# One layer of S5, block attention, memory attention and a conv FFN on one core: two PSUM banks each for scores and transposes, another order of the attention loop, and S5 parts behind projection tiles

## The chip, the core and the metric

The program runs on one core of one Trainium2 chip. The metric is the device time of one execution in microseconds, as the median of several runs. TensorE (PE) multiplies, its weight loads are listed apart as PEld, VectorE is DVE, ScalarE is ACT, GpSimd is POOL, SyncE (SP) issues most transfers. The granted TensorE clock was 1.00 of full speed over the whole execution.

## What is computed

Everything is fp32, for 512 tokens of width 1024. The reference, cut to what matters here:

```python
def reference(x, mem, ...):
    h = x
    hn = rms_norm(h, norm_mix)
    proj = hn @ w_in                       # u (512) | q | k | v (each 8 heads x 64)
    q, k = rms_norm(q, attn_qn), rms_norm(k, attn_kn)
    y_ssm = s5_mixer(u, ...)               # 32 groups x 16 channels, state 64, complex diagonal
    y_att = moba_attention(q, k, v, rel_bias)
    mixed = concat([rms_norm(y_ssm, gnorm_ssm), rms_norm(y_att, gnorm_attn)])
    h = h + mixed @ w_out
    h = h + memory_cross_attention(rms_norm(h), rms_norm(mem), ...)   # 4 heads x 128, 256 memory rows
    h = h + conv_ffn(rms_norm(h), ...)     # width 2816, causal depthwise conv of 3, silu gate

def s5_mixer(u, ...):
    # s[t] = ab * s[t-1] + bb @ u[t] ;  y = Re(c @ s) + d * u
    y = gelu(y)
    return y * sigmoid(y @ w_glu + b_glu)
```

With 512 tokens and blocks of 256, all earlier blocks are selected, so moba_attention is causal attention with a bias by distance bucket.

## The kernel before

Five programs are written out by hand, one for each engine (sync, gpsimd, scalar, vector, tensor). Each runs in its written order; semaphores hold them together. No scheduler moves anything.

**Weights.** They arrive in chunks of 1 MB (two units) in two raw buffers. ACT rounds a unit to its high part (`split_hi`, line 485), DVE forms the rest (`split_lo`, line 496, counted by the semaphore `lo_done`), into a ring of four units. A product of 128x128 by 512 columns is three matmuls (lines 513 to 515). The small fp32 matmuls of S5 and attention are line 1771, transposes on PE line 1774. `A_` (line 882) is any activation on ACT; `tt` and `stt` (lines 1253, 1259) are two-operand operations on DVE. A chunk is fetched into a raw buffer once both halves of the units in it are done.

**PSUM.** `plan()` (lines 273 to 328) names every use of the eight banks in order with `use(bank, name)`. PE's `fill(name)` waits until the bank's previous use was drained, the readers' `read(name)` until it is full. Before, scores of head step s (`sc{s}`) go round banks 3, 4 and 5; the transposed probabilities (`pt{s}`) of all steps, and the row factors `rl{t}`, use bank 6; attention's values (`pv{t}`) use bank 7. Banks 0, 1 and 2 hold the memory projections (`mk`, `mv`), the four pieces of the GLU product (`z0` to `z3`), and the output pieces `g{t}{half}` in bank (2t + half) mod 3. So g00 is in bank 0 and g01 in bank 1.

**S5.** The recurrence is cut into chunks of eight tokens. For each quarter q of the groups PE does `states_in(q)` (needs u, written to HBM and gathered back: semaphore `u0_in`), `kernels_in(q)` (needs a table of powers that POOL makes in `ca_table(q)`, line 804: `ca_ready`) and later `outputs(q, a)`. They stand between the projections of q, k and v, `proj(u, ...)`, each of four tiles (`proj_tile`, six matmuls of 512 columns). On POOL a chain of small operations on the S5 parameters opens the program; ca_table(0) ends it. DVE's `split_lo(0)` is ahead of its copy of the transposed parameters (`lam`), on which PE's next transposes wait.

**Attention.** There are 32 head steps, s = 8t + head, in tiles t of 128 query rows. For step s PE makes scores (`scores(s)` does s and s+1), DVE adds the bias and takes the extremum (`logits`, line 1555), ACT takes the exponential into `pbuf` (`probabilities`), PE transposes it in t+1 blocks (`prob_transposes`), ACT (even s) or DVE (odd s, line 383) copies that to SBUF (`pt_evac`), and PE multiplies with v (`values(s)` does s and s+1). PE's loop takes two steps at a time, a pair. At the head of a pair other work is inserted: `mv_tile` (memory values, up to s=6), `glu_half` (s = 8, 10, 12, 14: z0 to z3), and from s=16 pieces of the first half of the output projection (`sout_piece`, table `SOUT_AT`). ACT takes tanh of z{m} at s-1 = `GLU_AT[m]`; DVE makes the gated y (`y2`) at s-2 and its low part (`lo_of`) at s-4, ACT its high part and square at s-3. POOL sums squares. At step 19 these sums are reduced on PE, and DVE turns them into the root-mean-square factor (`mean_sq`, `root("ss")`). `g_residual(n)` on DVE scales g{t}{half} by it, adds it to the residual stream (which needs its transfer, `h_in`) and frees the bank. `G_ADD_AT` gives the steps of the first six. `SPLIT_AT` gives the steps at which weight units are split.

Of the kernel before, what the change touches and what calls it, by code (L numbers as in the profile page):

```python
# [20 lines left out]
TT = T // 128  # L21
# [5 lines left out]
H, HD = 8, 64  # L27
# [21 lines left out]
for _n, _k in GAINS:  # L49
# [14 lines left out]
SS_AT, MK_ROWS_AT = 19, 2  # L64

SOUT_AT = [(16, 0, 0), (16, 0, 1), (18, 1, 0), (20, 0, 2), (20, 0, 3), (22, 1, 2), (22, 1, 1), (24, 1, 3), (24, 2, 0),
           (26, 2, 2), (26, 2, 1), (28, 2, 3), (28, 3, 0), (30, 3, 1), (30, 3, 2), (30, 3, 3)]
G_ADD_AT = [21, 21, 23, 25, 27, 29]

# [31 lines left out]
def layer(nc, A, out):  # L101
# [10 lines left out]
    with ctx:  # L112
# [160 lines left out]
        def plan():  # L273
# [21 lines left out]
            for s in range(TT * H):  # L295
                if s >= H and s % H == 0:
                    use(6, f"rl{s // H - 1}")
                use(3 + s % 3, f"sc{s}"); use(6, f"pt{s}")
            for t in range(TT):
                use(7, f"pv{t}")  # L300
            use(6, "rl3"); use(6, "sa")
            use(0, "mk0"); use(1, "mk1"); use(0, "mv0"); use(1, "mv1")
            use(2, "z0"); use(0, "z1"); use(1, "z2"); use(2, "z3")
            use(5, "kx0"); use(3, "kx1")
            for t in range(TT):
# [376 lines left out]
        def _(pool):  # L682
# [36 lines left out]
            def ts(o, a, s1, s2, o1, o2):  # L719
                return nc.gpsimd.tensor_scalar(o, a, s1, s2, o1, o2)  # L720

            c = lambda i: sp[:, i, :]
            ab_re, ab_im, a_im = pw[:, 0, :, 1], pw[:, 1, :, 1], lam[:, GP:2 * GP]
# [149 lines left out]
        def _(act):  # L873
# [222 lines left out]
            mem_rows("mk", mkrow, 0)  # L1096
            probabilities(0)
            y_out(3)
            mem_rows("mk", mkrow, 1)
            for s in range(TT * H):  # L1100
                if s % 2 == 1:
                    pt_evac(act, lambda o, i: A_(o, i, ACT.Copy), s - 1)
                if s + 1 < TT * H:
                    probabilities(s + 1)
                if s >= H and s % H == 0:
                    factors_in(s // H - 1)
# [135 lines left out]
        def _(dve):  # L1242
# [103 lines left out]
            def turns(step):  # L1346
# [10 lines left out]
                if step == 3:  # L1357
# [6 lines left out]
                          lsrow[:, :].unsqueeze(2).to_broadcast([GP, 2, NS])).then_inc(step_row, 1)  # L1364
            split_lo(dve, 0)
            p = read(dve, "lam")
# [3 lines left out]
            x_half_lo(0, LOW)  # L1370
            x_half_lo(0, HIGH)
            split_lo(dve, 1)
            x_half_lo(1, LOW)
# [188 lines left out]
            for s in range(TT * H):  # L1562
# [7 lines left out]
                if s == SS_AT + 1:  # L1570
                    drained(V.tensor_copy(ev(sq, "ss"), p[:, 384:384 + TT]), f"pt{SS_AT}")
                    after_drain(dve, f"pt{SS_AT}")
                    mean_sq("ss")
                if s > H and s % H == 2:
                    ya_scale(s // H - 1)
# [13 lines left out]
                if s - 2 in GLU_AT:  # L1589
                    m = GLU_AT.index(s - 2)  # L1590
                    after_drain(dve, f"z{m}")
                    stt(yT[:, m, :], sg[:, m, :], 1.0, yT[:, m, :], ALU.add, ALU.mult).then_inc(y2_ready, 1)
                if s == SS_AT + 2:
                    root("ss")
                    dve.wait_ge(h_in, 16 * TT)
                for n, at in enumerate(G_ADD_AT):
# [172 lines left out]
        def _(pe):  # L1769
# [215 lines left out]
            proj(5, U_Q, "q")  # L1985
            states_in(0)
            kernels_in(0)
            proj(6, U_Q, "q")
            proj(7, U_Q, "q")
# [24 lines left out]
            for t in range(TT):  # L2014
                proj_tile(14, U_V, "v", t)
                outputs(2, t)
            weights_in(3)
# [125 lines left out]
            for s in range(0, TT * H, 2):  # L2143
# [7 lines left out]
                for at, t, i in SOUT_AT:  # L2151
                    if at == s:
                        sout_piece(t, i)
                if s >= H and s % H == 0:
                    factors(s // H - 1)
                if s + 2 < TT * H:
                    scores(s + 2)
                prob_transposes("pt", "sc", s, s // H + 1, 4)
                if s >= 2:
                    values(s - 2)  # L2160
                prob_transposes("pt", "sc", s + 1, s // H + 1, 4, s + 1 != SS_AT)
# [201 lines left out]
```

## Time and profile before

| | us |
|---|---|
| median of 3 runs | 717.7 (717.35 to 719.49) |
| the profiled execution | 719.06 |
| its span in the trace | 717.5 |
| PE busy | 698.7 |
| DVE busy | 423.7 |
| ACT busy | 308.0 |
| POOL busy | 130.7 |

A row of a timeline gives the start in us from the start of the span, the duration, engine and line, operation, result<-operands, the shape, how many like operations it groups, and in brackets how long the engine was idle just before, and on what it waited. A matmul's duration contains its fill and drain, so the cost of one in a row of them is the distance between two starts. A shape such as 64\*128 is the part of the array that the matmul uses.

In time the program goes: loading and transposing of x and the parameters to 13, projection and S5 to about 160, the attention loop to about 250, the output projection and memory attention, and from about 370 the FFN.

### The profile page before, as it was taken

The page shows a single profiled execution, that of the slowest core. Times are in us where ns is not written, and L with a number is a line of the kernel's source. Part 1 is how long each engine was busy: PE and PEld are TensorE (multiplying, and loading weights), DVE is VectorE, ACT ScalarE, POOL GpSimd, SP SyncE. Part 2 cuts the span into 40 slices and gives each one's busy share as a digit, 9 for nine tenths or more (in the row PEclk, how much of TensorE's full clock was granted, in tenths as well). Part 3 has the DMA queues.
Part 4 walks back from the last instruction along what each step waited for, and adds up shares of the span by engine and source line. Part 5 has one row for each costly group of instructions (what it writes and reads, how often), then busy time and mean ns, then how long its engine had stood idle before and what let it go on. Part 6 is the DMA issues. An engine that isn't in the chain of part 4 may idle for free.

```text
span 717.5 us, 10849 instructions
## 1 busy us (share of the span) xinstructions
PE 698.7 (97%) x3913; PEld 576.6 (80%) x3913; DVE 423.7 (59%) x710; ACT 308.0 (43%) x515; POOL 130.7 (18%) x134
## 2 busy tenths in 40 slices
PE   8999999998999999999999999999999999999998
PEld 7968887885676887878898888888888887888886
DVE  4998957737576567684856555554555574333333
ACT  5736444457664546253654333334333442232220
POOL 2999975023031110100200000000000000000000
PEclk9999999999999999999999999999999999999999
DMA  8645433266410033011124232232232332331203
GB/s 250 215 130 124 149 104 106 66 215 212 169 59 1 1 147 112 7 59 59 60 65 155 74 117 91 84 117 76 99 117 65 111 117 66 111 117 60 115 1 117
DMA packets 62999, 73.95 MB, mean 103 GB/s; under 512 B 20873, under 2 KB 47796, under 8 KB 62836
## 3 DMA queue, kind: packets, MB, share of 16 engines
q1 hardware_dynamic: 59172, 66.12, 28.4%
q10 hardware_dynamic: 3792, 7.36, 3.2%
q8 instruction: 22, 0.36, 0.2%
q14 instruction: 13, 0.11, 0.0%
HBM read 68.08 MB, written 5.78 MB: 103 GB/s over the span
## 4 chain that ended last, share of the span: by engine, by line
PE 81%; DVE 5%; ACT 4%; POOL 4%; DMA 2%; issue 2%; SPq 2%; ACTq 0%; DVEq 0%; POOLq 0%
PE pb L513 24%; PE pb L515 23%; PE pb L514 23%; PE pb L1771 7%; PE pb L1774 4%; POOL F L691 2%; DMA raw<-in_w_in 1%; ACT F L882 1%; DVE F L1253 1%; SPq L616 1%; ACT xs L882 1%; DMA F<-scr_b 1%; DVE xs L1259 1%; DVE F L1259 1%; ACT wring L485 1%
## 5 line engine op out<-in xcount | busy, mean ns | idle before, releaser
L496 DVE TENSOR_TENSOR wring<-raw,wring 128x1024 fp32r<-128x1024 f32 x100 | 128.5, 1287 | 76.6 <-ACT wring L485 76.3
L513 PE MATMUL pb<-xs,wring 128*128 128x512 f32 (+1 forms) x448 | 165.1, 368 | 0.2 <-issue 0.2
L515 PE MATMUL pb<-xs,wring 128*128 128x512 f32 (+1 forms) x448 | 164.1, 366 | 0.0
L514 PE MATMUL pb<-xs,wring 128*128 128x512 f32 (+1 forms) x448 | 164.1, 366 | 0.0
L485 ACT ACTIVATE wring<-raw 128x1024 fp32r<-128x1024 f32 x100 | 105.0, 1054 | 88.2 <-PE pb L515 75.0
L1259 DVE SCALAR_TENSOR_TENSOR F<-pb,ccol,F 128x511 f32<-128x511 f32 x88 | 65.9, 749 | 103.4 <-ACT F L882 97.5
L513 PE MATMUL pb<-wring,bs 128*128 128x512 f32 x240 | 96.3, 401 | 2.1 <-ACT F L882 1.2
L513 PEld LDWEIGHTS pb<-xs,wring 128*128 128x128 f32 x448 | 84.5, 189 | 14.2 <-issue 0.6
L515 PEld LDWEIGHTS pb<-xs,wring 128*128 128x128 f32 x448 | 84.5, 189 | 13.6
L514 PEld LDWEIGHTS pb<-xs,wring 128*128 128x128 f32 x448 | 84.5, 189 | 13.6
L515 PE MATMUL pb<-wring,bs 128*128 128x512 f32 x240 | 93.6, 390 | 0.0
L514 PE MATMUL pb<-wring,bs 128*128 128x512 f32 x240 | 93.5, 390 | 0.0
L882 ACT ACTIVATE F<-pb,ccol 128x512 f32<-128x512 f32 x44 | 34.2, 778 | 121.4 <-PE pb L515 117.5
L513 PE MATMUL pb<-wring,xs 128*128 128x512 f32 x192 | 81.0, 422 | 2.4 <-DVE F L1259 1.6
L1771 PE MATMUL pb<-F 64*128 64x128 f32 (+7 forms) x864 | 73.9, 276 | 2.2 <-DMA F<-scr_u 1.2
L515 PE MATMUL pb<-wring,xs 128*128 128x512 f32 x192 | 75.3, 392 | 0.0
L514 PE MATMUL pb<-wring,xs 128*128 128x512 f32 x192 | 75.1, 391 | 0.0
L1771 PEld LDWEIGHTS pb<-F 64*128 64x128 f32 (+3 forms) x864 | 59.4, 157 | 15.6 <-issue 9.5
L882 ACT ACTIVATE F<-pb 128x256 f32<-128x256 f32 (+6 forms) x60 | 26.7, 470 | 69.8 <-PE pb L1774 52.1
L513 PEld LDWEIGHTS pb<-wring,bs 128*128 128x128 f32 x240 | 45.1, 188 | 12.8 <-ACT F L882 2.0
L515 PEld LDWEIGHTS pb<-wring,bs 128*128 128x128 f32 x240 | 45.0, 188 | 9.7
L514 PEld LDWEIGHTS pb<-wring,bs 128*128 128x128 f32 x240 | 45.1, 188 | 8.7
(142 smaller groups left out, 777.7 us busy)
## 6 DMA issues: line engine op xcount, KB each, us to landing
raw<-in_ffn_w_up SPq DMA_DIRECT2D x22, 1024.0 KB, 5.0
raw<-in_ffn_w_down SPq DMA_DIRECT2D x11, 1024.0 KB, 4.8
F<-in_x SPq DMA_DIRECT2D x8, 512.0 KB, 5.0
raw<-in_w_in ACTq DMA_DIRECT2D x4, 1024.0 KB, 5.7
raw<-in_w_out SPq DMA_DIRECT2D x4, 1024.0 KB, 5.3
raw<-in_w_in SPq DMA_DIRECT2D x3, 1024.0 KB, 5.9
raw<-in_x_wkv ACTq DMA_DIRECT2D x3, 1024.0 KB, 5.8
raw<-in_x_wq SPq DMA_DIRECT2D x2, 1024.0 KB, 5.2
```

Source lines behind the costliest of these rows:

```text
L485: ins = nc.scalar.activation(w_unit(u, 0), raw_unit(u), ACT.Copy)
L496: ins = nc.vector.tensor_tensor(w_unit(u, 1), raw_unit(u), w_unit(u, 0).bitcast(f32), ALU.subtract)
L513: nc.tensor.matmul(ps, lh, rh, start=first, stop=False)
L514: nc.tensor.matmul(ps, lh, rl_, start=False, stop=False)
L515: return nc.tensor.matmul(ps, ll, rh, start=False, stop=last)
L616: sync.dma_start(toep[d * CG:(d + 1) * CG, :, (L - 1 - d) * CG:], kt[0:CG, :, 0:(d + 1) * CG]).then_inc(t_in[q], 16)
L691: return nc.gpsimd.tensor_tensor(o, a, b, ALU.mult)
L882: return nc.scalar.activation(o, i, f, **k)
L1253: return V.tensor_tensor(o, a, b, op)
L1259: return V.scalar_tensor_tensor(out=o, in0=a, scalar=s1, in1=b, op0=o1, op1=o2)
L1771: return nc.tensor.matmul(o, l, r, start=start, stop=stop)
L1774: return nc.tensor.transpose(o, i, ident[0:i.shape[0], 0:i.shape[0]])
```

## The change

Six things are altered.

1. **Banks.** Scores go round banks 3 and 4, transposes round 5 and 6. mv0 is in bank 2 and mv1 in bank 0; z0 to z3 are in banks 1, 2, 0, 1; the memory keys' transposes are in 3 and 4. The g pieces keep their banks, so the use before g01 in bank 1 is now z3 (before: z2), and the one before g00 in bank 0 is z2 (before: z1).
2. **ACT** takes the exponentials of a pair directly after each other, at odd s.
3. **PE's pair**: values(s-2) and scores(s+2) come first behind the inserted work, then the factors, then both transposes.
4. **DVE** does root("ss") at s=20 instead of 21, and g00's and g01's residuals too.
5. **split_lo(0)** is done by POOL, at the head of its program.
6. **S5**: states_in(0) and kernels_in(0) come after the first tile of proj(6), outputs(2,0) after tile 1 of unit 14, directly ahead of outputs(2,1).

```diff
-G_ADD_AT = [21, 21, 23, 25, 27, 29]
+G_ADD_AT = [20, 20, 23, 25, 27, 29]
...
-                use(3 + s % 3, f"sc{s}"); use(6, f"pt{s}")
+                use(3 + s % 2, f"sc{s}"); use(5 + s % 2, f"pt{s}")
...
-            use(0, "mk0"); use(1, "mk1"); use(0, "mv0"); use(1, "mv1")
-            use(2, "z0"); use(0, "z1"); use(1, "z2"); use(2, "z3")
-            use(5, "kx0"); use(3, "kx1")
+            use(0, "mk0"); use(1, "mk1"); use(2, "mv0"); use(0, "mv1")
+            use(1, "z0"); use(2, "z1"); use(0, "z2"); use(1, "z3")
+            use(3, "kx0"); use(4, "kx1")
...
+            pool.wait_ge(hi_done, 1)
+            nc.gpsimd.tensor_tensor(w_unit(0, 1), raw_unit(0), w_unit(0, 0).bitcast(f32), ALU.subtract)\
+                .then_inc(lo_done, 1)
...
             probabilities(0)
+            probabilities(1)
             y_out(3)
...
-                if s + 1 < TT * H:
+                if s % 2 == 1 and s + 1 < TT * H:
                     probabilities(s + 1)
+                    probabilities(s + 2)
...
-            split_lo(dve, 0)
             p = read(dve, "lam")
...
+            dve.wait_ge(lo_done, 1)
             split_lo(dve, 1)
...
                     mean_sq("ss")
+                    root("ss")
+                    dve.wait_ge(h_in, 16 * TT)
...
-                if s == SS_AT + 2:
-                    root("ss")
-                    dve.wait_ge(h_in, 16 * TT)
...
-            states_in(0)
-            kernels_in(0)
-            proj(6, U_Q, "q")
+            for t in range(TT):
+                proj_tile(6, U_Q, "q", t)
+                if t == 0:
+                    states_in(0)
+                    kernels_in(0)
...
                 proj_tile(14, U_V, "v", t)
-                outputs(2, t)
+                if t == 1:
+                    outputs(2, 0)
+                if t >= 1:
+                    outputs(2, t)
...
-                if s >= H and s % H == 0:
-                    factors(s // H - 1)
-                if s + 2 < TT * H:
-                    scores(s + 2)
                 prob_transposes("pt", "sc", s, s // H + 1, 4)
-                if s >= 2:
-                    values(s - 2)
                 prob_transposes("pt", "sc", s + 1, s // H + 1, 4, s + 1 != SS_AT)
```

(The added lines of the last piece stand ahead of the two transposes: values(s-2), scores(s+2), factors.)

What PE runs behind the output pieces of the pair s=16, before (scores are the rows with a result of 128x128 from F, values those with 64x128, the row factors the transposes of F, the transposes of step 16 and 17 those of pbuf):

```order
L1774 MATMUL pb<-ident,F 128x128 [waits bank_free6,rlrow_ready]
L1774 MATMUL pb<-ident,F 128x128 x3
L1771 MATMUL pb<-F 128x128 [waits bank_free4,bank_free3]
L1771 MATMUL pb<-F 128x128 x5
L1774 MATMUL pb<-ident,pbuf 128x128 [waits bank_free6,bank_free4]
L1774 MATMUL pb<-ident,pbuf 128x128 x2
L1771 MATMUL pb<-F 64x128 [waits bank_free6]
L1771 MATMUL pb<-F 64x128 x3
L1774 MATMUL pb<-ident,pbuf 128x128 [waits bank_free6,bank_free5]
L1774 MATMUL pb<-ident,pbuf 128x128 x2
```

and after:

```order
L1775 MATMUL pb<-F 64x128 [waits bank_free6,bank_free5]
L1775 MATMUL pb<-F 64x128 x3
L1775 MATMUL pb<-F 128x128 [waits bank_free4,bank_free3]
L1775 MATMUL pb<-F 128x128 x5
L1778 MATMUL pb<-ident,F 128x128 [waits bank_free6,rlrow_ready]
L1778 MATMUL pb<-ident,F 128x128 x3
L1778 MATMUL pb<-ident,pbuf 128x128 [waits bank_free5,bank_free3]
L1778 MATMUL pb<-ident,pbuf 128x128 x2
L1778 MATMUL pb<-ident,pbuf 128x128 [waits bank_free6,bank_free4]
L1778 MATMUL pb<-ident,pbuf 128x128 x2
```

The values moved from between the two transposes to the front, and wait for the drains of both banks of transposes; the two transposes stand together and fill different banks.

ACT around s=13 to 15, before (the exponentials write pbuf and lsum, the tanh of z2 and z3 are the ones with hbglu):

```order
L882 ACTIVATE F<-pb6 128x256 [waits bank_full6,pv_done]
L882 ACTIVATE pbuf,lsum<-pb5,nmx 128x256 [waits logit_ready,bank_full5,bank_full6]
L485 ACTIVATE wring<-raw 128x1024 [waits bank_full0,raw_in0]
L882 ACTIVATE F<-pb1,hbglu 128x512 [waits bank_full1]
L882 ACTIVATE xs<-F,gcol 128x512 [waits y2_ready]
L882 ACTIVATE F<-F 128x512
L882 ACTIVATE pbuf,lsum<-pb3,nmx 128x256 [waits logit_ready,bank_full3,bank_full6]
L882 ACTIVATE F<-pb6 128x256 [waits bank_full6,pv_done]
L882 ACTIVATE pbuf,lsum<-pb4,nmx 128x384 [waits logit_ready,bank_full4,bank_full6]
L882 ACTIVATE F<-pb2,hbglu 128x512 [waits bank_full2]
```

and after:

```order
L885 ACTIVATE F<-pb5 128x256 [waits bank_full5,pv_done]
L885 ACTIVATE pbuf,lsum<-pb3,nmx 128x256 [waits logit_ready,bank_full3,bank_full5]
L885 ACTIVATE pbuf,lsum<-pb4,nmx 128x256 [waits logit_ready,bank_full4,bank_full6]
L485 ACTIVATE wring<-raw 128x1024 [waits bank_full2,raw_in0]
L885 ACTIVATE F<-pb0,hbglu 128x512 [waits bank_full0]
L885 ACTIVATE xs<-F,gcol 128x512 [waits y2_ready]
L885 ACTIVATE F<-F 128x512
L885 ACTIVATE F<-pb5 128x256 [waits bank_full5,pv_done]
L885 ACTIVATE pbuf,lsum<-pb3,nmx 128x384 [waits logit_ready,bank_full3,bank_full5]
L885 ACTIVATE pbuf,lsum<-pb4,nmx 128x384 [waits logit_ready,bank_full4,bank_full6]
L885 ACTIVATE F<-pb1,hbglu 128x512 [waits bank_full1]
```

Each odd step now has two exponentials, and the tanh of z3 (last row) stands behind both of its step; it reads bank 1.

PE at the end of proj(5), before:

```order
L1771 MATMUL pb<-F 64x64 [waits bank_free5,bank_free4,u0_in]
L1771 MATMUL pb<-F 64x64 x7
L1771 MATMUL pb<-F 64x64 [waits bank_free5]
L1771 MATMUL pb<-F 64x64 x7
L1771 MATMUL pb<-F 16x128 [waits bank_free7,bank_free6,ca_ready]
L1771 MATMUL pb<-F 16x128 x15
L513 MATMUL pb<-wring,xs 128x512 [waits lo_done]
```

and after:

```order
L513 MATMUL pb<-wring,xs 128x512 [waits lo_done]
L514 MATMUL pb<-wring,xs 128x512
L515 MATMUL pb<-wring,xs 128x512
L513 MATMUL pb<-wring,xs 128x512
L514 MATMUL pb<-wring,xs 128x512
L515 MATMUL pb<-wring,xs 128x512
L1775 MATMUL pb<-F 64x64 [waits bank_free5,bank_free4,u0_in]
L1775 MATMUL pb<-F 64x64 x7
L1775 MATMUL pb<-F 64x64 [waits bank_free5]
L1775 MATMUL pb<-F 64x64 x7
L1775 MATMUL pb<-F 16x128 [waits bank_free7,bank_free6,ca_ready]
L1775 MATMUL pb<-F 16x128 x15
```

Six matmuls of 512 columns, one tile, moved ahead of the states and kernels.

## Rows read from the trace of the kernel before

**Rows 1.** the page's busy line (engine, us, share of the span, instructions).

```profile
PE 698.7 (97%) x3913; PEld 576.6 (80%) x3913; DVE 423.7 (59%) x710; ACT 308.0 (43%) x515; POOL 130.7 (18%) x134
```

**Rows 2.** PE's waits by releaser: total us, times, longest.

```profile
PE pb L1774 <- ACT F L882: 2.9, 6, 1.0
PE pb L513 <- DVE F L1259: 2.0, 2, 1.6
```

**Rows 3.** PE's timeline, S5 part: start, us, operation, count, [idle before <-releaser].

```profile
50.88 0.39 PE L515 MATMUL pb<-wring,xs 128*128 128x512 f32 x1
52.45 1.15 PE L1771 MATMUL pb<-F 128*64 128x64 f32 x32 [1.18 <-DMA F<-scr_u]
53.83 1.92 PE L1771 MATMUL pb<-F 64*16 64x128 f32 x32 [0.23 <-POOL F L804]
...
122.25 0.39 PE L514 MATMUL pb<-wring,xs 128*128 128x512 f32 x1
122.48 0.40 PE L515 MATMUL pb<-wring,xs 128*128 128x512 f32 x1
123.47 1.22 PE L1771 MATMUL pb<-F 128*128 128x64 f32 x12 [0.59 <-DVE bs L1259]
```

**Rows 4.** POOL's timeline, last of ca_table(0).

```profile
51.50 2.28 POOL L804 TENSOR_TENSOR F<-F 128x576 f32<-128x576 f32 x1
```

**Rows 5.** the start: DVE, PE, POOL, ACT; last, POOL's halves grouped (min/median/max ns).

```profile
10.13 1.23 DVE L496 TENSOR_TENSOR wring<-raw,wring 128x1024 fp32r<-128x1024 f32 x1 [4.40 <-ACT wring L485]
...
11.52 1.75 PE L1774 MATMUL pb<-ident,F 128*128 128x128 f32 x14 [0.82 <-DVE lam L1367]
...
14.99 1.05 POOL L720 TENSOR_SCALAR sp<-sp 128x16 f32<-128x16 f32 x1
...
16.06 1.28 ACT L882 ACT_TABLE_LOAD   x1
...
L828 POOL TENSOR_TENSOR xs<-F,xs x4: 1274/1280/1297, 157.6 to 178.5; 128x512 fp32r<-128x512 f32 x4
```

**Rows 6.** PE's timeline in the attention loop.

```profile
163.10 0.50 PE L513 MATMUL pb<-wring,bs 128*128 128x512 f32 x1 [1.18 <-ACT F L882]
...
179.36 0.47 PE L513 MATMUL pb<-xs,wring 128*128 128x512 f32 x1
...
185.36 0.41 PE L1774 MATMUL pb<-ident,pbuf 128*128 128x128 f32 x2 [1.02 <-ACT F L882]
...
189.09 0.44 PE L1774 MATMUL pb<-ident,pbuf 128*128 128x128 f32 x2
189.46 0.66 PE L1771 MATMUL pb<-F 128*64 128x128 f32 x8
190.15 0.41 PE L1774 MATMUL pb<-ident,pbuf 128*128 128x128 f32 x2
190.32 0.47 PE L513 MATMUL pb<-xs,wring 128*128 128x512 f32 x1
...
205.21 0.52 PE L1774 MATMUL pb<-ident,pbuf 128*128 128x128 f32 x3 [0.78 <-ACT F L882]
...
220.32 0.50 PE L513 MATMUL pb<-wring,xs 128*128 128x512 f32 x1 [1.56 <-DVE F L1259]
```

**Rows 7.** DVE's timeline in the attention loop.

```profile
177.91 0.28 DVE L383 COPY F<-pb 128x128 f32<-128x128 f32 x1
...
198.10 1.76 DVE L1259 SCALAR_TENSOR_TENSOR F<-F 128x512 f32<-128x512 f32 x1
199.78 1.21 DVE L496 TENSOR_TENSOR wring<-raw,wring 128x1024 fp32r<-128x1024 f32 x1
```

**Rows 8.** ACT's timeline in the attention loop.

```profile
195.15 1.06 ACT L485 ACTIVATE wring<-raw 128x1024 fp32r<-128x1024 f32 x1
...
201.64 0.58 ACT L882 ACTIVATE pbuf<-pb,nmx 128x384 f32<-128x384 f32 x1 [1.82 <-DVE nmx L1555]
202.21 0.68 ACT L882 ACTIVATE F<-pb,hbglu 128x512 f32<-128x512 f32 x1
```

More of the change, by code:

```diff
@@ L2153, in _ @@
                         sout_piece(t, i)
+                if s >= 2:
+                    values(s - 2)
+                if s + 2 < TT * H:
+                    scores(s + 2)
                 if s >= H and s % H == 0:
                     factors(s // H - 1)
-                if s + 2 < TT * H:
-                    scores(s + 2)
                 prob_transposes("pt", "sc", s, s // H + 1, 4)
-                if s >= 2:
-                    values(s - 2)
                 prob_transposes("pt", "sc", s + 1, s // H + 1, 4, s + 1 != SS_AT)
```

## The prediction

> **What bounds the kernel now.** I first read the page's busy line [rows 1]: PE is busy 698.7 of the span's 717.5 us. So only two things can move the time: PE's idle (the other 18.8 us) and what PE pays for its own order. Next I read PE's waits grouped by releaser [rows 2]: behind the start, the largest groups wait for ACT (2.9 us) and for a DVE sum (2.0). Then I read PE's timeline at each of those waits, to see which instruction is late and who is behind it. Two places matter. In the S5 part PE stands still for 1.18 us ahead of the states, 0.23 ahead of the kernels and 0.59 ahead of outputs(2,0) [rows 3]. In the attention loop it waits 1.18, 1.02, 0.78 and 1.56 us [rows 6]; smaller ones are in the 2.9 of [rows 2]. The stretch behind the loop (the FFN above all) is untouched. Durations are from the profiled execution (719.06 us, span 717.5); the sum is a difference and is laid on the median of 717.7, 1.4 us below that execution. A measurement of this kernel can tell about 0.3% (2.15 us) from no change.
>
> **S5 parts behind tiles.** Before, states_in(0) stands at PE's front from 51.27 to 52.45, waiting for the gathered u [rows 3]. After, the six products of tile (6,0) go first. One costs 0.23 us from start to start (122.25 to 122.48, [rows 3]), so the tile is 1.37 us; it ends at 52.6 and the wait is filled. The states (1.15 us) then end at 53.8, when ca_table on POOL has just finished (51.50 + 2.28 = 53.78, [rows 4]), so the 0.23 goes too. Saved: 1.18 + 0.23 = 1.41, less the 0.03 by which the tile overshoots the wait: **−1.38**. What hides it is a tile whose operands lie ready; if POOL came later by x, x less 0.2 would come back. The later outputs(2,0) now stands behind tile (14,1), whose 1.37 us cover the 0.59 of [rows 3] and the 0.17 by which the step (122.48 to 123.47) further exceeds a product's 0.23. One change of tile shape less gives at most 0.15 more: **−0.76 to −1.0**, I take −0.92, near its upper end because outputs(2,0) and (2,1) now follow each other. Evacuations of these parts move with PE. S5 together: **−2.3**.
>
> **split_lo(0) on POOL.** DVE's took 1.23 us and PE's next work waited 0.82 for the copy behind it [rows 5]. POOL's own subtractions of half that size take 1.28 [rows 5], so POOL needs some 2.55 from 10.1 to 12.65. DVE's lam copy then comes at once, and the first products could start about 0.3 earlier than 13.03, since they need POOL's result only in their third matmul. But POOL's parameter chain, whose first part ended at 14.99 + 1.05 = 16.04, then starts 0.75 us later. ACT loads its table from 16.06 to 17.34 [rows 5], and only then can it take that result: if the load does not wait for it, the 0.75 lies beside the load. PE meets two points that do not move with it, u at 52.4 and ca_table at 53.8, and the 0.3 is lost there: **0**. Bounds: −0.3, and +0.75 if POOL's whole chain moves, since the kernels then wait for POOL. A rule of the Trainium skill speaks against this part: page "SBUF — State Buffer", section "Who interferes with whom", says that a VectorE instruction with two SBUF inputs contends with a GpSimd instruction that reads SBUF, and the loser waits. No run here shows that pair of instructions yet; by this rule POOL's subtraction would end later than 12.65, and what it adds comes on top of the 0.75.
>
> **Attention: the early steps.** Giving mv1 bank 0 instead of 1 takes away the 1.18 at 163.10 [rows 6], since nothing that ACT is still to read is in it. With two banks for transposes the second transpose of a pair no longer waits for the evacuation of the first. But values(s−2) now open the block behind the products, and need the evacuation of pt(s−1). For values(4) that is DVE's copy at 177.91, which ends at 178.19 [rows 7], behind skip_in(3) and split_lo(25); values(4), scores(8), two transposes of step 6 and of 7 follow (about 1.3 us). The pair of s=8 thus starts at about 179.4, as before (179.36, [rows 6]). All gain up to there, some 2 us, is given back: **0**. From s=8 to 14 the waits of 1.02 [rows 6] and the cheaper order count: PE is 1.0 ahead at s=16.
>
> **The cheaper order.** Two transposes in front of values take 0.37 us (189.09 to 189.46), and the same two in front of full products 0.17 (190.15 to 190.32) [rows 6]. With pt(s) directly ahead of pt(s+1), a pair pays that exit once less: 0.15 (if half of the difference is an overlap that returns elsewhere, 0.1; at most 0.2), in about 15 pairs −2.2. Part of it stands in the 1.0 at s=16. The Trainium skill's page "TensorEngine Tiling (Array Packing)", Key Properties, says that changing the tiling mode drains TensorE; [rows 6] agree with some 0.2 us. By that rule values to scores is still a change, so a pair keeps three of four; were all four charged alike, the saving would be the same one of 0.15 to 0.2.
>
> **The new wait.** The second piece at s=16 fills bank 1. Before, its last reader was the tanh of z2; after, that of z3. On ACT that tanh (202.21 before, [rows 8]) stands at s=15 behind pt_evac(14), prob(16) and now also prob(17). Going through the queues: PE finishes pt(13) at 194.3; ACT does prob(14), prob(15), split_hi(28) (1.06, [rows 8]), tanh z2 and the first xs to 198.0; DVE follows with lo_of (0.7), y2 (1.76 beside POOL, [rows 7]), split_lo(28) (1.21, [rows 7]) and both logits to 202.6; ACT's two exponentials and the tanh (0.58 + 0.58 + 0.68, [rows 8]) end at 203.7 to 204.5. PE, 1.0 ahead, wants the bank at 200.6. Wait: **3.1 to 3.9, I take 3.4**. It replaces the 0.78 at 205.21 [rows 6] and one of 0.2 behind it, as both probabilities are then done. So at s=18: −1.0 + 3.4 − 1.0 = +1.4; a wait of values(16) for step 17's evacuation, bounded by 0 and the 0.78 at 205.21, adds 0.6 (nearer to that row, as its copy too stands behind logits): +2.0.
>
> **The early root.** g11 at 220.32 waited 1.56 for g00's sum on DVE, which stood behind the root at s=21 [rows 6]; moved to s=20 it is in time, with 0.16 more as the step shrinks: −1.72, leaving +0.3. Behind it DVE's queue holds the logits(22), 1.5 us later, which nobody wants before 216. The pairs from s=22 on give five times 0.15, less 0.2 for a transpose bank behind rl: −0.55. **Attention: −0.3.** Behind the loop nothing changes. Sum: −2.3 − 0.3 = **−2.6, or 715.1 us**.
>
> **Rivals.**
>
> *A, the early gain lasts.* If DVE's queue before 177.91 moves forward with PE (its split_lo(25) waits for ACT, which is freed by the 1.18, and not for the transfer that skip_in(3) needs), the 2.0 us at s=8 stay, and every later time comes 2.0 sooner, the new wait's too. If y2 also takes the 0.75 that DVE's other 512-column sums take, and not 1.76, the new wait is 1.0 shorter: −2.6 − 2.0 − 1.0 = −5.6, 712.1. For it: the whole loop is driven from PE. Against: the copy of [rows 7] ends a queue that DVE works off without a gap from 173.6.
>
> *B, the pair chain becomes the bound, and it is slower.* Scores, both logits, both exponentials, both transposes now go as one group; in pairs 16 to 22 ACT and DVE also carry squares, xs, y2, the root and two residuals. Each of three pairs then waits 1.7 us more, the length of one y2 [rows 7]: +5.1 − 2.6 = +2.5, 720.2. It decides from 0.87 a pair (2.6/3). For it: the 0.78 at 205.21 shows PE already waiting for ACT there [rows 6]; against: between 206.8 and 218.6 PE waits for neither of them.
>
> *C, the S5 gain fails* because split_lo(0) delays POOL's chain by 0.75 or more up to ca_table: S5 −0.5, sum −0.8, 716.9. For it: POOL's chain was on the path (0.23, [rows 3]); against: the table load's cover.
>
> *D, the edit doesn't do what it says* (the order stays in effect because every second bank waits for the same reader): −2.3 from S5 alone, 715.4, within the forecast's own range.
>
> **How the numbers follow.** Forecast with D 0.56, A 0.15, C 0.15, B 0.14. The forecast's own range is 713.0 to 717.3: S5 ±0.5, the bank wait −0.3/+0.5, the order ±0.7, values(16) ±0.4. To leave out no more than 2 in 10, the range goes down past A's 712.1 by its own half-width, to 710.9, and up to part of B, 719.2. Faster by over 0.3% is below 715.55: A's 0.15 and 0.34 of the forecast: 0.49. Slower is above 719.85: 0.09 of B, whose middle is 720.2, and 0.05 for the upper tails of C and of the forecast: 0.14. The same: 0.37.
>
> **What would show it.** Tile (6,0) from 51.0 and no idle ahead of the states or kernels; outputs(2,0) without idle; mv1 without its 1.18; s=8 at the old time less S5's gain; a wait of 3 to 4 us for ACT at the second piece of s=16; no 1.56 at g11. Wrong if POOL's ca_table ends after 54.0, if the bank wait is under 1 or over 6 us, or if new waits stand ahead of values in many pairs.

## The result and the profile after

The changed kernel takes **722.23 us** (median of 9 runs, 720.21 to 724.75), the kernel before 718.02 (9 runs beside it). The ratio is **1.0063**, with a 95% interval of 1.0050 to 1.0076: slower by 4.5 us, where 2.6 us less was forecast and the range ended at 719.2. The profiled execution has a span of 721.7 us, against 717.5. One execution of the kernel before, beside the last four experiments, took 1153.44 us at a mean granted clock of 0.558; it stands in no ratio here.

The S5 part went as planned. These rows of PE's timeline answer to [rows 3]: PE does the tile, the states follow with no idle, and the kernels wait 0.15 us for POOL instead of 0.23; outputs(2,0) and (2,1) run as one group of 24 with no idle ahead of them, where 0.59 was.

```profile
52.02 0.39 PE L515 MATMUL pb<-wring,xs 128*128 128x512 f32 x1
52.34 1.15 PE L1775 MATMUL pb<-F 128*64 128x64 f32 x32
53.65 1.92 PE L1775 MATMUL pb<-F 64*16 64x128 f32 x32 [0.15 <-POOL F L807]
...
122.52 2.33 PE L1775 MATMUL pb<-F 128*128 128x64 f32 x24
```

POOL's last operation of ca_table(0), which answers to [rows 4], ends at 53.59:

```profile
51.31 2.28 POOL L807 TENSOR_TENSOR F<-F 128x576 f32<-128x576 f32 x1
```

Where PE waits now (the view of its waits by releaser, as [rows 2]: total us, times, longest):

```profile
PE pb L1775 <- DVE F L383: 4.8, 4, 1.6
PE pb L513 <- ACT F L885: 3.7, 1, 3.7
PE pb L1778 <- ACT F L885: 1.5, 4, 0.6
PE pb L1775 <- DVE F L1258: 1.4, 1, 1.4
```

The old entries are gone or smaller: 1.18 ahead of mv1, 1.02 at s=8, 1.56 at g11 [rows 6]. In their place stand 4.8 us for DVE's copy of transposed probabilities (line 383), 1.4 us for a DVE product (line 1258) and one wait of 3.7 us for ACT. PE's timeline in the loop places them; 202.66 is the second output piece at s=16, and the rows of line 1775 with a wait are all values:

```profile
168.93 0.86 PE L1775 MATMUL pb<-F 128*64 128x128 f32 x8 [0.92 <-DVE F L383]
...
174.53 1.08 PE L1775 MATMUL pb<-F 128*64 128x128 f32 x12 [1.60 <-DVE F L383]
...
176.20 0.63 PE L514 MATMUL pb<-xs,wring 128*128 128x512 f32 x1
176.62 0.63 PE L515 MATMUL pb<-xs,wring 128*128 128x512 f32 x1
...
179.70 0.39 PE L514 MATMUL pb<-xs,wring 128*128 128x512 f32 x1
179.93 0.40 PE L515 MATMUL pb<-xs,wring 128*128 128x512 f32 x1
...
202.66 0.47 PE L513 MATMUL pb<-wring,xs 128*128 128x512 f32 x1 [3.72 <-ACT F L885]
...
211.89 1.74 PE L1775 MATMUL pb<-F 128*64 128x128 f32 x24 [1.37 <-DVE F L1258]
...
224.13 1.97 PE L1775 MATMUL pb<-F 128*64 128x128 f32 x28 [0.83 <-DVE F L383]
...
231.08 1.97 PE L1775 MATMUL pb<-F 128*64 128x128 f32 x28 [1.41 <-DVE F L383]
```

One thing in these rows is no wait. Two products of 512 columns start 0.42 us apart at 176.20 to 176.62, and 0.23 apart at 179.70 to 179.93. The view by stretches tells why (columns: from:to, us, busy us and instructions of PE, of its weight loads, of DVE, ACT and POOL, then granted clock, DMA share, GB/s):

```profile
172.00:175.50 3.50, 1.90 (x17) 1.17 (x15) 2.38 (x4) 1.57 (x2) 1.77 (x2) 1.00 1.01 379
175.50:179.30 3.80, 3.80 (x14) 2.98 (x12) 1.09 (x6) 3.16 (x7) 1.12 (x2) 0.55 1.02 415
198.00:202.50 4.50, 0.94 (x5) 0.42 (x3) 3.45 (x8) 1.79 (x6) 0.98 (x2) 1.00 0.00 0
202.90:206.80 3.90, 3.90 (x22) 2.63 (x23) 2.44 (x2) 0.75 (x2) 1.32 (x1) 0.56 0.02 4
```

The clock granted to TensorE is 1.00 up to 175.5, 0.55 from there to 179.3, and 1.00 again behind it; and 0.56 from 202.9 to 206.8. Those are the two levels, 2.4 and 1.2 GHz, with the edges of the stretch mixed in. Each time PE had stood still just before: it was busy for 1.90 of the 3.5 us before the first fall (after 0.92 and 1.60 us of waiting), and for 0.94 of 4.5 before the second (3.72). In the kernel before the whole span has 1.00, though it too waits 1.56 at one place [rows 6].

Put against the old timeline, the pair of s=0 starts 2.43 us earlier than before (156.19, before 158.62), s=2 4.85, s=4 5.17, s=8 3.6 earlier (175.74, [rows 6] 179.36), s=10 2.5, s=16 2.85 earlier (197.28, before 200.13). Then s=18 is 2.1 late, s=20 3.4, s=26 3.7, s=30 3.4, and the end 4.2.

### The profile page after: what moved, and what is told of

The parts are those of the page before. It is cut to its first block, busy times and chain, and to the rows that moved or that the text cites. A ratio compares the mean times of both kernels' runs of the same rounds, so it can differ in the third digit from the quotient of the medians.

```text
span 721.7 us, 10851 instructions
## 1 busy us (share of the span) xinstructions
PE 700.1 (97%) x3913; PEld 579.3 (80%) x3913; DVE 422.9 (59%) x709; ACT 308.3 (43%) x515; POOL 132.8 (18%) x135
## 4 chain that ended last, share of the span: by engine, by line
PE 81%; DVE 7%; ACT 4%; POOL 4%; issue 2%; DMA 1%; SPq 0%; ACTq 0%; DVEq 0%; POOLq 0%
PE pb L513 24%; PE pb L515 23%; PE pb L514 23%; PE pb L1775 8%; PE pb L1778 4%; POOL F L691 2%; DVE F L1258 1%; DMA raw<-in_w_in 1%; DVE wring L496 1%; ACT F L885 1%; ACT pbuf L885 1%; DVE wring L499 1%; ACT xs L885 1%; DVE xs L1264 1%; ACT wring L485 1%
## 5 line engine op out<-in xcount | busy, mean ns | idle before, releaser
L1775 PE MATMUL pb<-F 64*128 64x63 f32 (+7 forms) x864 | 73.6, 278 | 6.5 <-DVE F L383 4.8
```

The costliest lines, as they stand in the source:

```text
L1775: return nc.tensor.matmul(o, l, r, start=start, stop=stop)
```

## The experiments

All are timed against the kernel before on the same chip, side by side; its median was 717.7 us beside the first eight experiments and 718.7 beside the last four. The changed kernel was not timed again beside them, so a distance "less than the changed kernel" is a difference of medians from 722.23, and good to about 1 us; where it matters the difference of the ratios is given. Two theories stood at the start. **Theory 1**: the wait for the tanh of z3, and the clock behind it, are the loss. **Theory 2**: PE's new order in a pair closes a loop through DVE, and that loop is the loss.

**The S5 parts alone.** Part 6 put into the kernel before:

```diff
-            states_in(0)
-            kernels_in(0)
-            proj(6, U_Q, "q")
+            for t in range(TT):
+                proj_tile(6, U_Q, "q", t)
+                if t == 0:
+                    states_in(0)
+                    kernels_in(0)
...
-                outputs(2, t)
+                if t == 1:
+                    outputs(2, 0)
+                if t >= 1:
+                    outputs(2, t)
```

> The kernel before, with part 6 alone (states_in(0) and kernels_in(0) behind the first tile of proj(6), outputs(2,0) behind tile 1 of unit 14). If the S5 gain is real and lasts to the end, the span is 2.3 us shorter than before, about 715.4 as a median, with no idle of PE ahead of the states and of outputs(2,0). Rival: attention's waits (1.18, 1.02, 0.78, 1.56) grow by what PE gained, since they are set by ACT and DVE, and the end moves by under 1 us.

Measured: 715.57 us, ratio 0.9972 (0.9960 to 0.9983), so 2.0 us. It lasts to the end: the rows of attention moved forward as a block, with the same waits:

```profile
181.18 0.41 PE L1774 MATMUL pb<-ident,pbuf 128*128 128x128 f32 x2 [1.02 <-ACT F L882]
...
201.15 0.52 PE L1774 MATMUL pb<-ident,pbuf 128*128 128x128 f32 x3 [0.78 <-ACT F L882]
...
216.25 0.50 PE L513 MATMUL pb<-wring,xs 128*128 128x512 f32 x1 [1.55 <-DVE F L1259]
```

They are 1.02, 0.78 and 1.55, at times 4.1 us ahead of [rows 6]. Of the 4.1, 0.9 is where this execution began (10.62 against the 11.52 of [rows 5]); the block of the last mk and first mv products starts 3.2 ahead (155.43, before 158.62), so 2.3 are the S5 parts'; and that block, up to the scores, took 0.96 less in this execution (5.11 us from 155.43 to 160.54, before 6.07 from 158.62 to 164.69), 0.67 of it at mv1's wait (0.51, before 1.18). The waits that were left did not grow, so the rival is out.

**split_lo(0) on POOL, added to that** (parts 5 and 6):

> The same, and split_lo(0) on POOL too (parts 5 and 6). If part 5 is worth nothing, the time is that of s5_only within 0.4 us; if POOL's chain is late by 0.75, PE waits ahead of the kernels and the time is up to 0.75 longer; if the earlier start lasts, 0.3 shorter.

Measured: 714.75 us, 0.9964 (0.9951 to 0.9977), 0.6 us better than s5_only by the ratios, within both intervals. POOL took 2.37 us for the subtraction. Its parameter chain then began at 11.77, where s5_only has 11.07, but the operation behind ACT's table load ran at 17.04, where s5_only has 16.98: the load hid all but 0.06 of the 0.70. DVE's group of eight operations, whose first ran beside the subtraction, took 3.22 us, in s5_only 3.23. Whether the gain of the start lasts cannot be told at this resolution; no cost shows.

So everything else, parts 1 to 4, costs 722.2 − 714.8 = 7.5 us (7.1 by the ratios), where the forecast had them at −0.3.

**PE's old order in a pair**, the rest as changed:

```diff
-                if s >= 2:
-                    values(s - 2)
-                if s + 2 < TT * H:
-                    scores(s + 2)
                 if s >= H and s % H == 0:
                     factors(s // H - 1)
+                if s + 2 < TT * H:
+                    scores(s + 2)
                 prob_transposes("pt", "sc", s, s // H + 1, 4)
+                if s >= 2:
+                    values(s - 2)
                 prob_transposes("pt", "sc", s + 1, s // H + 1, 4, s + 1 != SS_AT)
```

> The changed kernel with PE's old order in a pair (factors, scores, transposes of s, values, transposes of s+1), everything else as changed. If the waits ahead of values (1.0 and 1.6 at s=4 and 6, 1.4, 0.8 and 1.4 from s=18 on) come from values standing first, they shrink to under 0.5 each, the first clock dip at 175 to 179 us goes with them (1.6 us), and a pair costs 0.15 more: about 3 us faster than the changed kernel. If the waits are set by DVE's queue whatever PE does, they stay, at the second transposes, and the time is the changed kernel's plus 1 to 2 us.

Measured: 714.59 us, 0.9958 (0.9945 to 0.9972). That is 7.6 us faster than the changed kernel, more than twice what was expected. Without the order of part 3 none of the loss is left, and what it costs is larger than the waits ahead of values that it shows (6.1 us). The profiled execution of this kernel is its slowest (720.46 us, seven of the other eight are between 714.36 and 715.28): a transfer of the S5 outputs came late in it, DVE stood for it 2.46 us, PE 4.20 behind that, and the clock fell there, and again behind the wait for the tanh. That wait is still 3.15 us.

**The bank of g01.** First with g{t}{half} in bank (2t + half + 2) mod 3, so that g01 follows z2:

```diff
-                    use((2 * t + half) % 3, f"g{t}{half}")
+                    use((2 * t + half + 2) % 3, f"g{t}{half}")
```

> The changed kernel with one edit: the pieces g of the output projection go in bank (2t + half + 2) mod 3, so that g01 follows z2 in its bank, as in the kernel before, and no longer z3. Theory 1 (the wait for the tanh of z3 makes PE stand still for 3.7 us, and the clock granted to PE falls behind it): the wait goes, the clock stays at 1.00 around 203 to 207 us, and the time falls by 4 to 5.5 us against the changed kernel, to about 717 to 718. Theory 2 (the chain through logits, exponentials, transposes and values is the bound from s=16 on): the same time is lost in later waits ahead of values, and the time falls by under 1.5 us.

Measured: 729.35 us, 1.0158 (1.0133 to 1.0184), 7 us worse. The experiment brought a wait of its own, at 261.39: the first piece behind the loop now fills the bank of g30, which DVE empties late. A second fall of the clock goes with it: the granted clock is 0.50 from 260.0 to 266.5.

```profile
200.43 1.53 PE L1775 MATMUL pb<-F 128*64 128x128 f32 x20 [1.26 <-DVE F L383]
...
207.77 2.29 PE L1775 MATMUL pb<-F 128*64 128x128 f32 x24 [2.54 <-DVE F L1258]
...
261.39 0.77 PE L513 MATMUL pb<-wring,xs 128*128 128x512 f32 x1 [5.40 <-DVE F L1264]
```

and the stretch behind the second of its waits, by the view of stretches (the third number from the end is the granted clock):

```profile
208.50:219.50 11.00, 11.00 (x56) 8.91 (x52) 4.70 (x13) 2.13 (x6) 3.24 (x5) 0.53 0.21 88
```

But it shows two things. The wait for the tanh is gone, and PE waits for DVE instead, 1.26 us at s=16 and 2.54 at s=18. And behind these the clock is at half for 11 us. So the test was repeated with a bank for each piece that leaves the end of the loop alone:

```diff
-                    use((2 * t + half) % 3, f"g{t}{half}")
+                    use([2, 0, 1, 2, 0, 2, 1, 0][2 * t + half], f"g{t}{half}")
```

> The changed kernel with the banks of g00 to g31 set to 2, 0, 1, 2, 0, 2, 1, 0: g01 follows z2, and the first piece behind the loop (bank 2) does not wait for g30, which cost 5.4 us in g_banks. Theory 1 (the one wait for the tanh of z3 is what the change lost): the time falls by 4 us or more against the changed kernel, to 718 or less. Theory 2 (PE is held once a pair by a loop through DVE: values(s-2) stand ahead of scores(s+2) and need the copy of step s-1, which DVE does behind the logits of the scores before): PE then reaches the values of s=16 early and waits there and at s=18, 1.3 and 2.5 us as in g_banks, so under 1.5 us are gained, about 721.

Measured: 719.83 us, 1.0032 (1.0020 to 1.0044): 2.4 us less than the changed kernel, between both theories, and with the waits that theory 2 named. The larger of them, 2.54, is not for the copy itself: its releaser is the DVE product of line 1258, of which more below. Behind it the clock is 0.53 from 208.0 to 211.5.

```profile
174.10 1.08 PE L1775 MATMUL pb<-F 128*64 128x128 f32 x12 [1.62 <-DVE F L383]
...
199.58 1.53 PE L1775 MATMUL pb<-F 128*64 128x128 f32 x20 [1.30 <-DVE F L383]
...
206.92 2.35 PE L1775 MATMUL pb<-F 128*64 128x128 f32 x24 [2.54 <-DVE F L1258]
```

**Scores ahead of values**, which opens the loop and keeps both transposes together:

```diff
-                if s >= 2:
-                    values(s - 2)
                 if s + 2 < TT * H:
                     scores(s + 2)
+                if s >= 2:
+                    values(s - 2)
```

> The changed kernel with scores(s+2) ahead of values(s-2) in a pair, both transposes still together. Theory 2 (the loop through DVE): scores no longer wait for DVE's copy of step s-1, so the waits ahead of values at s=4, 6, 18, 22 and 24 (1.0, 1.6, 1.4, 0.8, 1.4 us) fall to under 0.5 each, the cheaper order is kept, and only the wait of 3.7 us for the tanh of z3 is left: 717 or less. Theory 1: those waits only moved there from the late bank; the time stays within 1.5 us of the changed kernel's 722.2.

Measured: 718.69 us, 1.0012 (1.0000 to 1.0024), 3.5 us less. From s=18 on, the waits ahead of values shrank from 1.37, 0.83 and 1.41 to one of 0.35, with a new one of 0.55 for an exponential ahead of the scores of s=18. The two early ones did not go, as had been expected: 1.04 and 1.15 are left (before 0.92 and 1.60). There DVE's queue is late by itself: it works from 169.84 up to the copy that PE wants, which ends at 173.95, without a gap. The bank's 3.72 stands, and the clock is no better (0.993 to 0.998 in the ten runs), so these 3.5 us are the order's.

**One exponential a step on ACT**, as before the change:

```diff
-            probabilities(1)
...
-                if s % 2 == 1 and s + 1 < TT * H:
+                if s + 1 < TT * H:
                     probabilities(s + 1)
-                    probabilities(s + 2)
```

> The changed kernel with ACT's old order, one exponential a step. If the tanh of z3 is late because prob(17) stands ahead of it, the wait at s=16 shrinks from 3.7 by one exponential and what it waits for, to 2.5 to 3, and the time falls by 1 to 2 us; if pairing the exponentials is what makes the transposes stand together without a wait, new waits appear ahead of the transposes of the first step of a pair, and the time rises.

Measured: 717.95 us, 1.0003 (0.9992 to 1.0015), 4.3 us less than the changed kernel. The expected 1 to 2 us were too few: the wait went from 3.72 to 1.60, and the mean granted clock is 1.000 in 8 of 10 runs, where the changed kernel had it in one of 9. New waits of 0.2 to 0.64 us for an exponential stand ahead of scores. The two early waits are as in the changed kernel, 0.88 and 1.64, and PE did even less ahead of 175.5; yet here the clock stayed:

```profile
172.00:175.50 3.50, 1.65 (x13) 0.97 (x14) 2.38 (x4) 2.99 (x5) 2.10 (x2) 1.00 1.04 424
175.50:179.30 3.80, 3.80 (x26) 2.74 (x22) 1.09 (x6) 1.85 (x6) 1.11 (x2) 1.00 1.01 415
```

**Work in place of the wait.** This kernel does more than it needs: sixteen products whose result is thrown away.

```diff
+                    if (at, t, i) == (16, 0, 1) and s == 16:
+                        after_drain(pe, "z1")
+                        pe.wait_ge(ym_ready, 2)
+                        for n in range(16):
+                            mm(pb[2][:, :], x_tile(0, n % 2, 0), w_unit(U_OUT, 0)[:, n % 2, :])
                     if at == s:
                         sout_piece(t, i)
```

> The changed kernel with 16 additional products of 512 columns (3.6 us of PE work whose result is not used) just ahead of the second output piece at s=16, where PE stands still for 3.7 us. They replace idle time by work and save no wait. If PE standing still is what lowers the clock behind it, the dip at 203 to 207 us goes away and the time falls by some 1.5 us against the changed kernel, though PE does more; if the clock falls for another reason, the time is the same or up to 0.5 us longer.

Measured: 720.00 us, 1.0031 (1.0020 to 1.0041): **2.2 us faster with 3.8 us more of work**. Its timeline first, then the second stretch as above:

```profile
198.62 3.79 PE L1775 MATMUL pb<-wring,xs 128*128 128x512 f32 x16
202.51 0.47 PE L513 MATMUL pb<-wring,xs 128*128 128x512 f32 x1
202.82 0.40 PE L514 MATMUL pb<-wring,xs 128*128 128x512 f32 x1
203.05 0.39 PE L515 MATMUL pb<-wring,xs 128*128 128x512 f32 x1
```

```profile
202.90:206.80 3.90, 3.60 (x33) 2.58 (x31) 3.58 (x6) 1.19 (x4) 1.32 (x1) 1.00 0.02 4
```

The piece starts at 202.51, as late as before (202.66), so no wait was saved; but in the stretch in which the changed kernel had 0.56, the clock is 1.00, and products start 0.23 us apart. So PE's idle is what lowered it there. The Trainium skill's page "TensorE: Matmul & The Clock Gate", Part 1, says that the array's clock is gated by how busy it has recently been. The trace agrees here: with PE busy in the gap the fall is gone. A wait on TensorE can thus have two prices; that it need not is shown by one_exponential above. The first fall, at 175, has no filler and is still in this profile, but this is the slowest of the ten runs: eight of them have a mean clock of 0.999 or 1.000, which leaves no room for a fall in them.

**Both repairs together**, and then with each of ACT's and PE's old orders:

> The changed kernel with both repairs: scores ahead of values, and the bank table of g_table. If the late bank and the loop through DVE are the two causes and add up, 3.5 us (scores_first) and another 3 to 4 (the bank's wait of 3.7, with its clock dip) are gained: 714 to 716. If one hides the other, as the loop did in g_table, it is 717 or more, with new waits at s=18.

> Both repairs and ACT's old order of one exponential a step. If the pair of exponentials costs nothing once the bank is free in time, the time is that of scores_first_g within 0.5 us; if scores for the next pair need their bank before the second exponential is through (0.2 to 0.6 us a time in one_exponential), it is 1 to 2 us longer.

> The changed kernel with PE's old order in a pair and the bank table of g_table. In old_pe_order one wait of 3.2 us for the tanh of z3 was left in the loop. If it is the bank's alone, it goes, with its dip of the clock: 711 to 712.5. If ACT and DVE are late there anyway, PE waits at the transposes of s=16 and 17 instead, and it is 714.

scores_first_g measured 715.79 us, 0.9960 (0.9939 to 0.9981): 7.4 us less than the changed kernel by the ratios, and within the 714 to 716 of the expectation that the two causes add up. A part of the bank's wait came back at the scores of s=18, 1.79 us, for the exponential whose bank they fill; and 2.14 us ahead of values(4) are left, behind which the clock stayed at 1.00. scores_first_g_one measured 720.22 us, 1.0028 (1.0014 to 1.0042), 4.4 us more instead of at most 2: scores now stand at the front of the pair and need both exponentials, the second of which comes a step later, and the clock falls behind the longest of these waits.

```profile
176.12 1.74 PE L1773 MATMUL pb<-F 64*128 64x128 f32 x12 [2.23 <-ACT pbuf L885]
...
199.21 1.53 PE L1773 MATMUL pb<-F 64*128 64x128 f32 x20 [1.23 <-ACT pbuf L885]
...
211.89 1.75 PE L1773 MATMUL pb<-F 64*128 64x128 f32 x24 [1.66 <-ACT pbuf L885]
```

old_order_g measured **713.27 us**, 0.9943 (0.9920 to 0.9966), the lowest median of all and 4.1 us less than before by the ratio; its interval overlaps those of old_pe_order, s5_lo_pool and the next kernel, so it is not shown to be the best of them. Its expectation of 711 to 712.5 was just missed: in place of the 3.15 us are 1.10 for POOL ahead of the row factors of s=16 and 1.22 for an exponential ahead of the scores of s=18.

```profile
197.50 0.66 PE L1778 MATMUL pb<-ident,F 128*128 128x128 f32 x4 [1.10 <-POOL F L845]
...
203.17 0.94 PE L1775 MATMUL pb<-F 64*128 64x128 f32 x12 [1.22 <-ACT pbuf L885]
```

**The early root alone**, on top of parts 5 and 6 in the kernel before (part 4's edit as in the diff):

> The kernel before with parts 4, 5 and 6: the S5 parts, split_lo(0) on POOL, and root("ss") with the first two residuals at s=20. The wait of 1.55 us ahead of the second piece of g11 at s=22, left in s5_lo_pool, goes, and nothing else moves: 713.2 (s5_lo_pool's 714.75 less 1.6). Rival: DVE's logits(22) come later behind the root and two sums, and PE waits for them instead: 714.5.

Measured: 714.74 us, 0.9953 (0.9935 to 0.9971; before had 718.69 beside it). By the ratios 0.8 us better than s5_lo_pool, with intervals that overlap. The profile has no idle of PE between 204.1 and 278.6, so the 1.55 is gone and nothing took its place; how much of it reaches the end, 0.8 or 1.6, isn't settled.

## Why the prediction was wrong

**The S5 parts** were right: −2.3 forecast, −2.0 measured, tile (6,0) and tile (14,1) filled the waits, ca_table(0) ended at 53.59 with its slack. **split_lo(0)** as 0 was right within 0.6 us. (The prediction says that no run had shown VectorE beside a GpSimd instruction that reads SBUF; the 1.76 us that it takes for y2 from [rows 7] stood beside one.) Rival C is out.

**The early steps** were right in kind: the copy of step 5 held values(4), 1.60 us up to 174.53. But not all of the gain was given back: PE was 2.43 us early at s=0, 5.17 at s=4 and still 3.62 at s=8, so 1.2 of 2.7 us were left where 0 was forecast. The clock then took them: at s=16 PE is 2.85 early, 0.4 ahead of s=0 instead of the 1.0 of the forecast. What the step failed to say is that it puts two waits, 0.92 and 1.60, into 7 us. Rival A (the early gain lasts) is out: the half that was left at s=8 was gone at s=10, and y2 took 1.77.

**The new wait** was right in place and size: 3.72 us where 3.4 was taken, from 3.1 to 3.9. DVE's queue was the one told: y2 beside POOL's sum took 1.77 (0.68 for the y2 before it, without POOL), split_lo(28) 1.21, two logits, then ACT's two exponentials and the tanh. DVE's rows:

```profile
192.09 0.68 DVE L1264 SCALAR_TENSOR_TENSOR F<-F 128x512 f32<-128x512 f32 x1
...
197.15 1.77 DVE L1264 SCALAR_TENSOR_TENSOR F<-F 128x512 f32<-128x512 f32 x1
198.84 1.21 DVE L496 TENSOR_TENSOR wring<-raw,wring 128x1024 fp32r<-128x1024 f32 x1
199.98 0.55 DVE L1560 CUSTOM_DVE_ANT_0 pb<-pb,F 128x384 f32<-128x384 f32 x1
```

and ACT's, the two exponentials and the tanh of z3, which ends at 202.52:

```profile
200.71 0.58 ACT L885 ACTIVATE pbuf<-pb,nmx 128x384 f32<-128x384 f32 x1 [3.31 <-DVE nmx L1560]
...
201.28 0.57 ACT L885 ACTIVATE pbuf<-pb,nmx 128x384 f32<-128x384 f32 x1
...
201.83 0.69 ACT L885 ACTIVATE F<-pb,hbglu 128x512 f32<-128x512 f32 x1
```

**The first step that failed is what came behind it**: "a wait of values(16) ... adds 0.6", and then five pairs that give 0.15 each. Measured are 1.37 at s=18, 0.83 at s=22 and 1.41 at s=24, so new waits ahead of values in five pairs in all, one of the prediction's own signs of being wrong. I had looked at each value's copy singly, and at values(4) correctly, but did not see that the new order closes a cycle, which stands in every pair and held PE in those five of fifteen. In one turn of it, values(s−2) need DVE's copy of step s−1; that copy stands on DVE behind the logits of s and s+1 and all other work of that step; and since scores(s+2) now stand behind values(s−2), the next logits can't start before. PE and DVE then wait for each other in turns. DVE's rows around the second of the five show it:

```profile
169.82 0.30 DVE L1560 CUSTOM_DVE_ANT_0 pb<-pb,F 128x128 f32<-128x128 f32 x1 [1.04 <-PE pb L1775]
...
172.97 1.22 DVE L496 TENSOR_TENSOR wring<-raw,wring 128x1024 fp32r<-128x1024 f32 x1
174.10 0.28 DVE L383 COPY F<-pb 128x128 f32<-128x128 f32 x1
175.65 0.43 DVE L1560 CUSTOM_DVE_ANT_0 pb<-pb,F 128x256 f32<-128x256 f32 x1 [1.26 <-PE pb L1775]
```

DVE stands still for 1.04 us at 169.82 and for 1.26 at 175.65, waiting for PE's scores; PE stands still for 1.60 in between, up to 174.53, waiting for the copy at 174.10. With scores first (scores_first) DVE does its next logits at 173.87, directly behind that copy, without the 1.26; PE's wait shrinks to 1.15 only, so most of this one is the length of DVE's queue, and the order pays in full from s=18 on.

The wait at s=18 has one more link, which its releaser shows (line 1258 instead of 383). values(16) open attention tile 2 and fill bank 7, which DVE frees by scaling the values of tile 1, directly behind the copy of step 17:

```profile
209.46 1.23 DVE L496 TENSOR_TENSOR wring<-raw,wring 128x1024 fp32r<-128x1024 f32 x1 [1.02 <-ACT wring L485]
210.60 0.55 DVE L383 COPY F<-pb 128x384 f32<-128x384 f32 x1
211.07 0.68 DVE L1258 TENSOR_TENSOR F<-pb,F 128x512 f32<-128x512 f32 x1
```

The copy ends at 211.15, PE goes on at 211.89. The same link is the 2.54 us in g_table and g_banks. ACT has a part in the cycle as well: DVE had waited for it 1.02 us here, 1.67 shortly ahead of the copy that the values of the pair s=22 wanted, and 1.52 for those of s=24.

The saving of the cheaper order itself is real, and larger than the 0.15 forecast, so rival D (the edit has no effect) is out: a pair with two GLU halves and no wait took 4.79 us before (190.32 in [rows 6], the next at 195.11) and 4.55 after (187.56 to 192.11). The old order pays 0.24 us a pair and keeps the engines apart.

**The second is a term that the sum did not have**: the clock. Eight products at 0.43 instead of 0.23 us are 1.6 us at s=8; at s=16 the stretch from the late piece to the next pair took 6.24 us (202.66 to 208.90), with the filler 4.71 (202.51 to 207.22), so 1.5 more. In 9 runs the mean granted clock goes from 1.000 to 0.993, and the span with it: 718.6 us at 1.000, 719.4 to 720.6 at 0.997 and 0.998, 721.7 to 723.1 at 0.993 to 0.995. A mean of 0.998 is what one fall of 3.8 us at 0.55 leaves of 1.000 over such a span, and 0.995 two of them; the profiled run has two, the median run one. The one run at 1.000 took 720.21, so about 2 us of the median's 4.2 to 4.5 are the clock's, and the other 2.2 or so are what the waits cost beyond the gain of the S5 parts; the filler, which only puts work into a gap, gave 2.2 back. I had priced an idle microsecond at one microsecond.

**Rival B** (the pair chain becomes the bound, 720.2) had the right sign and a chain that binds in each pair. It placed it in the group of scores, logits, exponentials and transposes, at three pairs; the last link is DVE's copy (at s=18 the scaling behind it) ahead of values, at five pairs, and the paired exponentials made the tanh late. I gave it 0.14, since PE did not wait for ACT or DVE between 206.8 and 218.6 in the kernel before. That was no evidence: the old order was the reason why it did not, and with it back (old_pe_order) no such wait stands there.

What stays open: how the loss of 7.1 to 7.5 us divides between loop, bank and clock, as each repair also moves the others (by the ratios: scores first −3.7, bank −2.2, both −7.4, one exponential −4.3, old order −7.5); and why the clock fell in some executions of a kernel and not in others with the same waits. The kernel before is no exception: one of its 723.8 us had a mean clock of 0.993.

## What to carry to other kernels

Before moving an instruction forward on one engine, follow its operand to the engine that makes it, and ask what on that engine stands ahead of it and waits for something that is now behind the moved instruction: a cycle that goes round once per iteration makes both engines wait in turns, and the saving in the instruction stream doesn't show. A bank's next user waits for its last reader, so each new allotment of banks has to be read together with the order of the readers' engine. And a gap of several microseconds on TensorE can cost more than its length, so the granted clock behind it belongs to the reading.

## What the runs showed of the hardware

In profiled executions TensorE ran at half the clock around or behind waits: 3.9 us at 0.56 with one of 3.72, 3.8 us at 0.55 behind 0.92 and 1.60, 11 us at 0.53 behind 1.26 and 2.54 (g_banks), 6.5 us at 0.50 around one of 5.40 (g_banks). It did not behind 0.88 and 1.64 (one_exponential) or behind 2.14 (scores_first_g). Filling one gap with useless products made the kernel 2.2 us faster. A VectorE operation of 128x512 on two operands (y2) took 0.68 us alone and 1.77 beside a GpSimd operation of the same size. A GpSimd subtraction of 128x1024 took 2.37 us, where VectorE needs 1.23.
